# A fourth weight slot and a new order of modulation chunks in the projection stage of a decoder layer

## What is computed

```
sh1, sc1, gt1, sh2, sc2, gt2 = split(silu(c) @ w_ada + b_ada, 6)      # w_ada 1024 x 6144
h = rmsnorm(x, g_mix) * (1 + sc1) + sh1
z = h @ w_in + b_in                                                  # w_in 1024 x 5408
mq, mk, mv, mo, mi, mf, aq, akv, ag, ga, gb = split(z)
h_m, C, n, m = mlstm_chunkwise(mq, mk, mv, mi, mf, C0, n0, m0)         # 4 heads of 128
o_nsa = nsa(rmsnorm(aq), rope, rows of akv, paged cache, window)      # compressed, selected, window branch
x = x + gt1 * ((sigmoid(ga) * (sigmoid(mo) * h_m @ w_up_m) + sigmoid(gb) * (o_nsa @ w_up_a)) @ w_out)
x = x + gt2 * moe(rmsnorm(x, g_ffn) * (1 + sc2) + sh2)               # top 4 of 32 experts, clamped SwiGLU
```

## Time and profile before

| | |
|---|---|
| median of 3 runs | 1496.01 us (1492.72 to 1504.27) |
| the profiled execution, its own time | 1497.62 us |
| its span, first to last instruction | 1495.8 us |
| PE busy | 1387.6 us, 93% |
| DVE, ACT, POOL busy | 633.4, 321.0, 85.6 us |
| bytes moved by DMA | 501.73 MB, mean 335 GB/s |
| mean granted clock of TensorE | 0.98 |

### The profile page before, as it was taken

One profiled execution on the slowest core, in us unless ns is written; L12 is line 12 of the kernel. 1 busy time (PEld: TensorE's weight loads), 2 busy tenths in 40 slices (PEclk: granted clock), 3 DMA queues, 4 the chain that ended last, 5 costly groups with the idle time before them and its releaser, 6 DMA issues. The chain is left out here.

```text
span 1495.8 us, 21870 instructions
## 1 busy us (share of the span) xinstructions
PE 1387.6 (93%) x8444; PEld 658.3 (44%) x8444; DVE 633.4 (42%) x1575; ACT 321.0 (21%) x597; POOL 85.6 (6%) x126
## 2 busy tenths in 40 slices
PE   4998899999899889999999999999999999999997
PEld 2456577777777443333333333333333333333332
DVE  2165334467675545544433332333234233323334
ACT  3003132256552132111111111111111111111110
POOL 1300000222202100000000000000000000000001
PEclk9999999999999979999999999999999999999999
DMA  9875635354423949999999999999999999999994
GB/s 329 258 264 229 243 161 173 129 186 142 142 114 112 314 166 425 427 428 427 428 428 428 428 428 428 428 428 428 428 428 428 428 428 428 428 428 428 428 428 195
DMA packets 65475, 501.73 MB, mean 335 GB/s; under 512 B 6432, under 2 KB 12500, under 8 KB 40583
## 3 DMA queue, kind: packets, MB, share of 16 engines
q1 hardware_dynamic: 55056, 463.07, 74.9%
q0 software_dynamic: 10368, 37.97, 7.5%
HBM read 495.45 MB, written 9.15 MB: 337 GB/s over the span
## 5 line engine op out<-in xcount | busy, mean ns | idle before, releaser
L1187 PE MATMUL bank_v<-arena 128*64 128x512 f32 (+13 forms) x4916 | 821.4, 469 | 58.6 <-DMA arena<-in_w_gu 27.1
L1187 PEld LDWEIGHTS bank_v<-arena 128*64 128x64 f32 (+7 forms) x4916 | 333.1, 137 | 506.9 <-issue 351.7
L1187 PE MATMUL bank_s<-arena 128*64 128x512 f32 (+2 forms) x2004 | 425.7, 506 | 11.3 <-ACT arena L1084 6.6
L1187 PEld LDWEIGHTS bank_s<-arena 128*64 128x64 f32 (+2 forms) x2004 | 181.3, 143 | 224.6 <-issue 166.0
L965 DVE TENSOR_SCALAR arena<-bank_v 128x512 f32<-128x512 f32 x32 | 22.1, 692 | 374.8 <-PE bank_v L1187 374.8
L987 DVE TENSOR_TENSOR arena<-bank_v,arena 128x512 f32<-128x512 f32 x128 | 82.5, 686 | 122.7 <-PE bank_v L1187 122.7
L1081 ACT ACTIVATE arena<-arena 128x512 f32<-128x512 f32 x32 | 20.2, 630 | 394.1 <-DVE arena L965 394.1
L1191 PE MATMUL bank_s<-const_tables,arena 128*128 128x128 f32 (+3 forms) x605 | 94.0, 287 | 5.2 <-issue 2.9
L1191 PEld LDWEIGHTS bank_s<-const_tables,arena 128*128 128x128 f32 (+3 forms) x605 | 71.7, 170 | 55.6 <-issue 37.7
L1689 DVE TENSOR_TENSOR arena<-bank_v,arena 128x288 f32<-128x288 f32 (+10 forms) x128 | 49.5, 387 | 93.8 <-PE bank_v L1187 66.1
L992 DVE TENSOR_TENSOR x_rows<-x_rows,arena 128x512 f32<-128x512 f32 x128 | 82.8, 688 | 2.2
(11 more groups left out here) (122 smaller groups left out, 627.5 us busy)
## 6 DMA issues: line engine op xcount, KB each, us to landing
arena<-in_w_gu SPq DMA_DIRECT2D x128, 2048.0 KB, 24.0
arena<-in_w_dn SPq DMA_DIRECT2D x64, 2048.0 KB, 21.9
arena<-in_w_ada SPq DMA_DIRECT2D x12, 2048.0 KB, 11.9
arena<-in_w_in SPq DMA_DIRECT2D x10, 2048.0 KB, 13.4
arena<-in_state_win_kv POOLq DMA_DIRECT2D x8, 512.0 KB, 7.1
arena<-in_w_out SPq DMA_DIRECT2D x2, 2048.0 KB, 19.9
out_win_sample<-in_state_win_kv POOLq DMA_DIRECT2D x1, 4064.0 KB, 27.8
x_rows<-in_x_prompt POOLq DMA_DIRECT2D x4, 512.0 KB, 8.8
```

Source lines behind the costliest of these rows:

```text
L1187: return pe.matmul(out, l, r, start=first, stop=last)
```

## The change

A fourth slot, `SPARE`, is made of the 4096 words from `mq` on (`mq` and most of `C0h`), and `slot_of` becomes a written list. Column chunks 0 and 1 write `mq` and the state loads write `C0h`, so the chunks in this slot have to be done before: it takes row chunk 1, then the second halves of modulation chunks 4 and 5, and modulation chunk 5 moves ahead of column chunk 0. On PE modulation chunk 2 moves up behind column group 1 of chunk 1, and modulation chunk 3 ahead of the product `prompt_value(0)`, behind both `prompt_out`; DVE's stream follows. POOL's two state loads move behind `mod_ready`, 1, the first modulation store right behind them. SP waits for `rms`, 3 (the squares in `sqs`) before its fifth load, row chunk 1, and issues the bias loads behind that one. `gffn` moves to `pair`.

```
-STAGE1 = [("row", 1), ("row", 2), ("row", 3), ("ada", 4), ("row", 0), ("col", 0), ("ada", 5), ("col", 1), ("ada", 2), ("ada", 3)]
+STAGE1 = [("row", 1), ("row", 2), ("row", 3), ("ada", 4), ("row", 0), ("ada", 5), ("col", 0), ("col", 1), ("ada", 2), ("ada", 3)]
...
-        slot_of = [n % NW for n in range(FIRST_UP - 1)] + [2] + [0, 1, NW, NW + 1]
+        SPARE = NW + 2
+        slots.append(arena[:, mq.offset:mq.offset + WORDS])
+        slot_of = [0, 1, 2, 0, SPARE, 1, 2, 0, SPARE, 1, 0, SPARE, 2, 0, 1, 2, 1, 2] + [0, 1, 2, 0, 2] + [0, 1, NW, NW + 1]
...
-        gffn = arena[:, mq.offset + 4 * NTOK:mq.offset + 4 * NTOK + D]
+        gffn = pair
...
+            ada_part(5)
             col_chunk(0)
             turn_tile(2)
...
-            ada_part(5)
             pe.wait_ge(sem("pair_rows"), 16)
...
             col_group(1, 1)
+            ada_part(2)
             pe.wait_ge(sem("kc_squared"), 1)
...
             prompt_out(0)
-            ada_part(2)
-            prompt_value(0)
             prompt_out(1)
             ada_part(3)
+            prompt_value(0)
             prompt_value(1)
...
-            ada_part(2)
-            prompt_value(0)
             ada_part(3)
             v(ve.nop(), "mod_ready")
+            prompt_value(0)
             prompt_value(1)
...
-            state_in(0)
-            state_in(1)
...
             pool.wait_ge(sem("mod_ready"), 1)
+            state_in(0)
+            state_in(1)
             store_mod(4)
...
             for n in range(n1):
+                if n == 4:
+                    sp.wait_ge(sem("rms"), 3)
                 load(n)
-                if n == 3:
+                if n == 4:
                     for o_, i_ in row_bias:
```

More of the change, by code:

```diff
@@ L284, in program @@
         FIRST_UP = chunk_at[("up_m", 0)]
-        slot_of = [n % NW for n in range(FIRST_UP - 1)] + [2] + [0, 1, NW, NW + 1]
+        SPARE = NW + 2
+        slots.append(arena[:, mq.offset:mq.offset + WORDS])
+        slot_of = [0, 1, 2, 0, SPARE, 1, 2, 0, SPARE, 1, 0, SPARE, 2, 0, 1, 2, 1, 2] + [0, 1, 2, 0, 2] + [0, 1, NW, NW + 1]
+        assert len(slot_of) == FIRST_UP + 4
         def before_in_slot(n):
@@ L370, in program @@
         sqs = arena[:, mq.offset:mq.offset + D]
-        gffn = arena[:, mq.offset + 4 * NTOK:mq.offset + 4 * NTOK + D]
+        gffn = pair
+        assert mq.offset + WORDS <= n0r.offset
         at[0] = ARENA - 16 * NTOK
@@ L1868, in _ @@
             tt(gwc[0:4, :].unsqueeze(2), m0b, ML, sub, "gate_logs")
+            ada_part(5)
+            v(ve.nop(), "mod_ready")
             b = got("pages")
```

5 lines of the change are left out of this document (removed).

## The result

The changed kernel takes 1482.46 us (median of 4 runs, 1477.97 to 1487.67), the kernel before 1498.8 us beside it (median of 4, 1492.72 to 1504.27): the ratio is 0.9885, 95% interval 0.9847 to 0.9922, faster by 1.1% (an interval from 0.8 to 1.5%). The prediction said 1477 us, 1470 to 1489. The profiled execution took 1483.44 us (span 1481.6), against 1497.62 (1495.8): 14.2 us less where the sum said 19.9.

What follows compares the result with a forecast made beforehand. The prediction held that PE's waits for late weight chunks, and the slow clock behind them, bound the first stage. 2.9 + 5.0 + 5.5 + 7.2 - 0.7 = 19.9 us off gave 1477 us, range 1470 to 1489.

Steps and rivals of the forecast that it cites:

- the five waits for chunks: PE's waits before row chunks 1 and 0, column chunk 1 and both halves of modulation chunk 3, 18.4 us, would go.
- the rival of the small loads: SP's longer queue delays POOL's tables 7 us, DVE starts at 64.4, PE stands 3 us near 62: 1482 to 1487, chance 0.14.
- The upper bound of the start, 4.5 us: Most gained at row chunk 1's start, if modulation chunk 1's last half also lands earlier without the bias loads.
- Start, 2.9 us: Row chunk 1, issued ahead of the bias loads, starts on PE at about 37.8 us instead of 40.69: 2.9 us gained.
- the start at half clock stays: At row chunk 1, PE's slow clock at the start was taken as unchanged, with no gain or loss.
- Row chunk 0, 5.0 us: Its slot frees ten us earlier; the 3.31 us wait and 1.7 us of slow clock go: 5.0 us gained.
- Column chunk 1, 5.5 us: Issued near 106, needed at 125.2; the 3.84 us wait and 1.7 us of slow clock go: 5.5 us gained.
- What the moves cost: PE runs the same matmuls; DVE's bias add ahead of the value products holds the gate-column transposes: 0.7 us lost.
- Modulation chunk 3, 7.2 - 0.7 us: Waits of 3.10 and 2.84 us and 1.3 us of slow clock go, less 0.7 us for DVE's drain order.
- The gain is spent in the heads: Gates return no earlier, so PE stands 9.5 us for head 2's state: 1487; chance 0.17 together with waits that stay.
- The transfers become the bound: Mean rate in the first stage falls to 232 GB/s, so it takes 208.6 us: 1522 us, chance 0.03.
- The waits don't go: SP's queue order keeps chunks behind a late slot, halving the gain: 1487; chance 0.17 together with the gain spent in heads.

Runs made afterwards that it cites:

- both repeats: Changed kernel run twice more with no edit, each beside the kernel before: 1487.36 us, ratio 0.9904, and 1481.87 us, ratio 0.9877.
- the slot's experiment: Changed kernel's fourth slot and moved bias and state loads, but the chunk order of the kernel before: 1492.47 us, ratio 0.9954 to the kernel before.
- the order's: Kernel before with its three slots, given only the new order of chunks on SP, PE and DVE: 1500.89 us, ratio 1.0012.
- With PE kept busy: Changed kernel plus four unused 128 x 512 matmuls ahead of modulation chunk 1's last half, two behind its transposes: 1478.51 us, ratio 0.9874 to the kernel before.
- the last experiment: Changed kernel plus unused matmuls at the start (three ahead of the half) and stage end, and ACT's sigmoids moved later: 1472.0 us, ratio 0.9823 to before.

## Why the prediction was right, and where its sum was off

The time fell in the range and in the likelier case (faster by over 1%), 5.5 us above the value. The mechanism held: the five waits for chunks went, in this trace and in both repeats. The size is a closer thing. The kernel's three ratios are 0.9877, 0.9885 and 0.9904, so one of them would have fallen in the case "within 1%", and 1482.46 us is also a time that the rival of the small loads names (1482 to 1487); only the trace tells the two apart. The upper bound of the start, 4.5 us, does not come out of its terms, which give 2.9 + 1.2 = 4.1; the sum does not use it.

Term by term, from the first trace:

- **Start, 2.9 us: came to 0.2.** The step that failed is its second input: "DVE finishes their first half at 36.86 + 0.62 = 37.5". In the changed kernel that is 39.1:

```profile
38.48 0.62 DVE L1693 TENSOR_TENSOR arena<-arena 128x128 f32<-128x128 f32 x2
```

The half of modulation chunk 1 took 3.24 us instead of 1.93 and began 0.3 later. That it would go on at full clock was assumed, not bounded. What makes it slow stays open: with the same program up to there it took 1.93 us in the slot's experiment, where row chunk 1 began at 37.18, and with the old start of SP's stream it took 3.04 in the order's. Of the eight traces with four slots and nothing added there seven have the slow half, of the two with three slots one. So the loss here is bad luck in part, and no run shows that it is a cost of the change. And "the start at half clock stays" was too cheap: the stretch took 48.03 us instead of 46.90. The load itself came as said (in the changed kernel issued at 21.38 and landed 16.6 us later, at 38.0; 37.2 in the slot's experiment; "near 38" forecast). With PE kept busy both losses went: 1.93 and 44.95, the second in the two traces that show the stretch without a wait in it.
- **Row chunk 0, 5.0 us: 5.1.** The wait and the slow clock behind it went, as said.
- **Column chunk 1, 5.5 us: 4.0.** The wait for the load and, in this trace, the slow clock went, and 1.52 us of waiting for ACT came. In both repeats group 0 ran slowly behind that wait (5.80 and 5.81 us for 4.12), so there the 1.7 us of slow clock in the term were not gained. The step that failed is "What the moves cost: PE runs the same matmuls": the term asked what PE and SP run, and not what ACT does while modulation chunk 5 is on PE. The other terms say what is late next behind a wait that goes; this one looks at the chunk alone. The experiments settle the cause: the wait for ACT is absent with the old order, present with three slots and the new one, and gone when the sigmoids move.
- **Modulation chunk 3, 7.2 - 0.7 us: 6.5** to where the gates begin, with 1.4 us of slow clock in it (1.32 + 1.90 against 0.75 + 1.10). So without the slow clock it was 7.9, and the 0.7 for the drain order was too much or the blocks between gave it back; which of the two no run shows.
- **Not in the sum: the gates at the lower level, 1.7 us** (9.73 against 8.03). With the waits gone the sum takes the slow clock to be gone. The row 156.56 above speaks against it: column group 3 was slow in the kernel before with no wait ahead of it. 0.2 + 5.1 + 4.0 + 6.5 - 1.7 = 14.1, and 14.0 was measured there.

The Trainium skill says of this, in "TensorE: Matmul & The Clock Gate", Part 1, that the throttled state is the default and that activity releases it. The traces agree as far as the start goes (last half of modulation chunk 1 in 1.93 us in all three traces with matmuls added in the wait). At the gates they show that the busy time of the profile does not tell the two levels apart: PE was busy for 5.00 of 5 us from 165 to 170 us both in the changed kernel (0.50 granted) and with four matmuls added (1.00).

The rivals. *The small loads come later* was wrong in its price: the page table was there at 60.35, 3.0 us later than the earlier trace rows, of which 1.6 is POOL starting later behind the modulated rows; no step of PE waited for a bank near 62 us. In other runs it came as late as 63.3, and PE didn't wait either. Its cause is likely but not shown: from POOL's first issue to the page table it was 18.0 us before and 17.5 with the order alone, and 18.1 to 21.8 in the traces with four slots; the 18.1 is that of the slot alone, whose early SP queue is the changed kernel's. *The gain is spent in the heads*: POOL's request came 16 us earlier, PE never stood. The gain did shrink a little on the way, from 14.0 us at the gates to 13.6 at the expert stage. *The transfers become the bound*: they gave 287 GB/s for 168 us, nothing like the 232 of that case; only with the other losses gone, in the last experiment, transfers decide again, for 0.7 and 2.0 us. *The waits don't go* fell with the list of waits.

What stays open is the scatter behind the heads. From the end of the heads to the issue of the output weights the same code took 165.6 (changed kernel), 170.4 and 168.8 us (its repeats), and from there to the second expert 89.0, 88.1 and 84.3; in the kernel before it was 168.8 and 85.5. That moves a span by 3 to 5 us with no cause in the change, and is as large as the terms argued over here; no experiment tried it.

## What to carry to other kernels

Where a chunk of work on one engine is moved away from a place, look at what the others did beside it: a table load on ACT had hidden there for nothing. When waits are priced, price the clock of TensorE with them, at both ends: it was worth 5.5 us beside a forecast of 20 (1.3 in the half, 1.1 in the stretch, 1.4 + 1.7 at the gates). A few unused matmuls in a wait that is there anyway brought back the part at the start; at the gates that is not shown. Before a slow block is put down to a change, look for it in several traces and in programs that are the same up to that point. A slot and an order are judged together, as alone they gave 0.5% and nothing.

## What the runs showed of the chip that I had not expected

- The granted clock fell with PE busy nearly throughout: it was 0.50 at 165 to 170 us, and what PE had done before were transposes of 32 x 32, products with 4 rows, and a wait of 0.31 us. With matmuls of 128 x 288 between them it was 1.00 in both traces, but one trace without them has full clock too. The kernel before shows the same fall at another place: 0.72 at 157 to 163 us, PE busy for all 6 us, behind products of 64 x 15.
- The same code may or may not meet it: 8.03 us for the gates in one trace with nothing added there, 9.6 to 10.4 in seven; 1.93 us for the half of modulation chunk 1 with the slot alone, 3.24 to 3.36 in three traces of the changed kernel, which is the same program up to there.
- Three matmuls that ended before the load landed cost nothing (PE still stood 0.19 us for it); with four the last half began at 33.67 without a wait. The stretch of 45 us behind them was 1.4 to 3.1 us shorter. In the place without a wait four matmuls cost 2.4 us, and what they gave is not shown.
- A table load took 1.28 us, and with three sigmoids it put 1.52 us on PE's path. The Trainium skill gives the same duration for the load itself ("ScalarE: Activation LUTs", What ACT_TABLE_LOAD costs), and beside it a drain of about 1380 ns for every switch to a different set. This trace does not show the drain: the table load begins at 126.75, 0.02 us behind ACT's work of 126.23 + 0.50, and the sigmoids at 128.05, 0.02 us behind the load.
